# Conditioning products moved from TensorE to multiply-adds on VectorE, and the second upward piece by token blocks

## Chip, cores and metric

One core of one Trainium2 chip. The time is that of the program on the device, in microseconds (us), the median of several runs.

## What is computed

Two networks, one behind the other, on 256 tokens of width 1024, in float32. The first has a recurrent layer (a gated linear recurrence), an MLP, a layer of sparse attention with a latent key (an index score picks 64 keys a query), and a second MLP. The second is a hybrid layer (neighbourhood attention with context keys, a short convolution, a conformer branch), whose input is shifted and scaled by a vector computed from a condition `c`, and whose output is gated by one:

```
def sq_relu_mlp(h, w_up, w_down):
    return jnp.square(jax.nn.relu(h @ w_up)) @ w_down        # 1024 -> 4096 -> 1024

def modulate(x, cond, norm_g, w_ada, b_ada):
    shift, scale, gate = jnp.split(jax.nn.silu(cond) @ w_ada + b_ada, 3, axis=-1)
    ...
    return rms_norm_2(x, norm_g) * (1 + scale) + shift, gate

x = x + mix                                                  # in each layer of the first network
x = x + sq_relu_mlp(rms_norm(x, norm_mlp_g[layer]), mlp_w_up[layer], mlp_w_down[layer])
```

The conditioning is `silu(cond) @ w_ada`, a row vector of 1024 times a 1024 x 3072 matrix. It is needed for two conditions (tokens and context) for shift and scale, and for one (tokens) for the gate. It depends on nothing but the inputs, and its result is first used in the second MLP, where the context is normalised.

## The kernel before

All weights come from HBM in pieces of 1 MB ([128, 2048] in float32), in one order written out by hand (`order()`). SP's queue loads them into a ring of three buffers (`RAW`). Each piece is split into a rounded part `WH` (ScalarE, `high`, L1104) and the remainder `WL` (VectorE, `low`, L1708), in a second ring of four. TensorE multiplies in three products (high by high, high by low, low by high), so that the result keeps float32 accuracy: `columns_matmul` (L294 to L296, weights stationary, 256 tokens moving), `tokens_matmul` (L325 to L327, a block `t` of 128 tokens stationary) and `columns_wide` (L312, L314).

An MLP has 16 upward pieces of 256 hidden columns and 16 downward pieces. In iteration j TensorE makes upward piece j and adds downward piece j - 2 to four PSUM banks (`t`, `n`: token block and half of the columns). ScalarE copies (L1254), VectorE adds, squares and makes the remainder (L1960, L1964, L1970).

Between stages the residual is added (`residual`, L1742), its squares summed on ScalarE (`norm_square`, L1111), the mean square made on VectorE (`variance`, L1718) and raised to -0.5 on GpSimd (`power`, L2520), the block scaled (`norm_scaled`, L1727), transposed on TensorE (`norm_transposes`, L364, the *turning* of a token block) and split again (`norm_high` L1140 on ScalarE, `norm_low` L1736 on VectorE). `residual_norm` and `norm_stage` hold VectorE's and ScalarE's order of this.

The conditioning matrix is taken in twelve pieces of 1 MB, four before each of three stages: the first MLP, attention and the second MLP. TensorE multiplies them in plain float32 (`ada_matmul`, L392): the condition's 128 values, padded to 32 columns, are the stationary operand, and a piece's 2048 columns move in four products of 512 to four groups of 32 output partitions. Ten of the pieces pass through the ring `RAW`, two are loaded ahead into `AD`. A copy to `AR` and small products with a selecting matrix (`ada_columns`, L405) turn the row to columns, and VectorE adds the bias (`ada_out`).

The first upward piece of an MLP is multiplied by token blocks (`up_by_tokens`), so that block 0 can start before block 1 is normalised; its hidden tile must then be transposed (`S.turn`, L546). The others are multiplied by `columns_matmul` (piece 1) and `columns_wide`. `rows_last_two` writes the last sum of a stage, block by block. In attention, `dots` (L661) makes the index scores, and `key_weights` (L675, copied at L1355) transposes the key weights between them.

Of the kernel before, what the change touches and what calls it, by code (L numbers as in the profile page):

```python
# [18 lines left out]
def order():  # L19
# [31 lines left out]
    return p  # L51

# [33 lines left out]

AHEAD = [("ada", 1, 0), ("ada", 1, 1)]


def chunks():  # L90
    out, i, m, at = {}, 0, 0, 0
    for key, piece in order():
        whole = key[0] in ("ada", "ri")
        apart = key[0] == "ri" or key in AHEAD
        out[key] = Chunk(None if apart else i, None if whole else m, piece[0], at)
        i += 0 if apart else 1
        m += 0 if whole else 1
        at += 128 * WIDTH[piece[0]]
    return out
# [38 lines left out]
class Memory:  # L138
# [3 lines left out]
    def __init__(self, nc, stack):  # L142
# [30 lines left out]
        self.TB = self.tile("TB", [128, 2, 512])  # L173
        self.AD = self.tile("AD", [128, 2, 2048])

# [47 lines left out]
        self.CM = self.tile("CM", [128, 8, 32])  # L223
# [117 lines left out]
def rows_last_two(T, M, S, stage, keys, x, ks, xready):  # L341
# [40 lines left out]
def ada_matmul(T, M, S, g, i, bank):  # L382
    c = M.CH["ada", g, i]
    if (g, i) in ((1, 0), (1, 1)):
        T.wait_ge(S.ahead[i], 16)
        weights = M.AD[:, i, :]
    else:
        T.wait_ge(S.raw[c.r], 16 * (c.i // NRAW + 1))
        weights = M.RAW[:, c.r, :]
    for q in range(4):  # L390
        k = 4 * g + i if g < 2 else 2 * i + q // 2
        made = T.e.matmul(M.PS[bank][32 * q:32 * q + 32, :], M.CM[:, k, :], weights[:, q * 512:(q + 1) * 512],  # L392
                          start=i == 0, stop=i == 3)
    made.then_inc(*S.ada.tick(g, i))


def ada_columns(T, M, S, g, bank):
    T.wait_ge(*S.arow.at(0))
    T.wait_ge(*S.arow.at(g))
    T.wait_ge(S.rest, 16)  # L400
    sel, n = (("sel", 8), ("selg", 4), ("selg", 4))[g - 1] if g == 1 else ("selg", 4)
    which = (0, 1) if g == 1 else (0,)
    for m in range(4):
        for a in which:
# [110 lines left out]
def tensor_mlp(T, M, S, l):  # L515
# [33 lines left out]
    if l:  # L549
        T.wait_ge(*S.xl.at(k, 1, 0))  # L550
        ada_columns(T, M, S, 2, 6)
# [2525 lines left out]
```

## Time and profile before

| | |
|---|---|
| median of 3 runs | 880.0 us (879.88 to 880.57) |
| the profiled execution | 879.89 us, its span 878.1 us |
| TensorE busy | 872.1 us of the span |
| VectorE, ScalarE, GpSimd busy | 588.9, 467.0, 65.0 us |
| read from HBM | 162.92 MB, 187 GB/s over the span |
| conditioning products on TensorE (L392) | 96 records, between 94.3 and 394 us |

The span runs from the first to the last instruction; the execution's own time has 1.8 us around it. Busy times are those of engines that work side by side, so they do not add up. Matmuls of TensorE overlap in the records; the distance of their starts is what one costs in a full row.

### The profile page before, as it was taken

The numbers are of one execution on the slowest core, as the hardware profiler recorded it, in microseconds if no ns is written. First come the engines' busy times: TensorE is split into PE (matmuls) and PEld (weight loads), VectorE is DVE, ScalarE is ACT, GpSimd is POOL, SyncE is SP. The second block draws the span as 40 slices with busy tenths as digits, with TensorE's granted clock in tenths as the row PEclk, the third lists the DMA queues.
The fourth block names the chain that finished last, engine by engine and source line by source line (L and its number), as shares of the span: only waits on it lengthen the run. The fifth ranks groups of instructions, "written<-read, shape, count | busy, mean of one in ns | idle before, by whom it ended". The sixth has DMA issues, their size and how long they took to land.

```text
span 878.1 us, 13080 instructions
## 1 busy us (share of the span) xinstructions
PE 872.1 (99%) x5128; PEld 742.8 (85%) x5128; DVE 588.9 (67%) x981; ACT 467.0 (53%) x749; POOL 65.0 (7%) x71
## 2 busy tenths in 40 slices
PE   9999999999999999999999999999999999999998
PEld 7998788888887887679888888888898888878887
DVE  5969775555554495567648576564477898896874
ACT  6796554444433477646546544454467674444540
POOL 3010000000000045300000000031100000000000
PEclk9999999999999999999999999999999999999999
DMA  8635886665542644478537455520435355545431
GB/s 326 241 124 208 304 293 242 243 237 195 192 144 97 228 171 166 137 267 328 188 116 278 185 192 192 192 108 8 188 110 182 126 196 189 189 150 200 171 155 48
DMA packets 30447, 164.81 MB, mean 188 GB/s; under 512 B 3377, under 2 KB 9777, under 8 KB 12082
## 3 DMA queue, kind: packets, MB, share of 16 engines
q1 hardware_dynamic: 30384, 163.97, 51.2%
q8 instruction: 41, 0.67, 0.3%
q14 instruction: 20, 0.16, 0.1%
q10 hardware_dynamic: 2, 0.00, 0.0%
HBM read 162.92 MB, written 1.05 MB: 187 GB/s over the span
## 4 chain that ended last, share of the span: by engine, by line
PE 97%; ACT 1%; DMA 1%; DVE 0%; issue 0%; SPq 0%; DVEq 0%; ACTq 0%
PE ps L325 16%; PE ps L327 16%; PE ps L326 16%; PE ps L312 12%; PE ps L294 7%; PE ps L295 7%; PE ps L296 7%; PE ps L314 6%; PE ps L466 2%; PE ps L392 1%; PE ps L887 1%; PE ps L912 1%; PE ps L896 1%; DMA BI<-in_dbias_dram 1%; PE ps L364 1%; ACT LG L1372 1%
## 5 line engine op out<-in xcount | busy, mean ns | idle before, releaser
L1708 DVE TENSOR_TENSOR WL<-RAW,WH 128x1024 fp32r<-128x1024 f32 x258 | 304.2, 1217 | 86.1 <-ACT WH L1104 85.7
L1104 ACT CAST WH<-RAW 128x1024 fp32r<-128x1024 f32 (+1 forms) x264 | 262.6, 1044 | 77.0 <-PE ps L327 66.7
L294 PE MATMUL ps<-XA,WH 128*128 128x256 f32 x496 | 143.3, 289 | 0.1
L312 PE MATMUL ps<-XA,WH 128*128 128x512 f32 x448 | 140.6, 395 | 0.0
L296 PE MATMUL ps<-XA,WL 128*128 128x256 f32 x496 | 140.3, 283 | 0.0
L295 PE MATMUL ps<-XA,WH 128*128 128x256 f32 x496 | 140.3, 283 | 0.0
L294 PEld LDWEIGHTS ps<-XA,WH 128*128 128x128 f32 x496 | 95.0, 192 | 7.4 <-issue 6.5
L314 PEld LDWEIGHTS ps<-XA,WL 128*128 128x128 f32 x448 | 84.2, 188 | 19.6
L325 PE MATMUL ps<-WH,HTh 128*128 128x512 f32 x256 | 100.0, 390 | 0.0
L326 PE MATMUL ps<-WL,HTh 128*128 128x512 f32 x256 | 99.7, 389 | 0.0
L327 PE MATMUL ps<-WH,HTl 128*128 128x512 f32 x256 | 99.6, 389 | 0.0
L295 PEld LDWEIGHTS ps<-XA,WH 128*128 128x128 f32 x496 | 95.1, 192 | 0.4 <-issue 0.2
L296 PEld LDWEIGHTS ps<-XA,WL 128*128 128x128 f32 x496 | 95.0, 192 | 0.0
L314 PE MATMUL ps<-XA,WL 128*128 128x256 f32 x448 | 88.0, 278 | 0.0
L312 PEld LDWEIGHTS ps<-XA,WH 128*128 128x128 f32 x448 | 70.2, 189 | 2.0
L325 PE MATMUL ps<-WH,XA 128*128 128x512 f32 (+2 forms) x192 | 71.2, 371 | 0.2
L327 PE MATMUL ps<-WH,XA 128*128 128x512 f32 (+2 forms) x192 | 69.7, 363 | 0.0
L326 PE MATMUL ps<-WL,XA 128*128 128x512 f32 (+2 forms) x192 | 69.7, 363 | 0.0
L1254 ACT COPY RL<-ps 128x512 f32<-128x512 f32 x28 | 16.4, 587 | 89.9 <-PE ps L314 89.8
L1960 DVE TENSOR_TENSOR RL<-ps,RL 128x512 f32<-128x512 f32 x28 | 19.4, 692 | 65.6 <-ACT RL L1254 65.6
L327 PEld LDWEIGHTS ps<-WH,HTl 128*128 128x128 f32 x256 | 48.1, 188 | 10.2
L325 PEld LDWEIGHTS ps<-WH,HTh 128*128 128x128 f32 x256 | 48.0, 188 | 9.0
(272 smaller groups left out, 1293.2 us busy)
## 6 DMA issues: line engine op xcount, KB each, us to landing
RAW<-in_w_dram SPq DMA_DIRECT2D x139, 1024.0 KB, 4.8
RI<-in_w_dram SPq DMA_DIRECT2D x2, 1024.0 KB, 11.3
GB<-in_gb_dram SPq DMA_DIRECT2D x4, 512.0 KB, 5.7
AD<-in_w_dram SPq DMA_DIRECT2D x2, 1024.0 KB, 6.8
BI<-in_dbias_dram SPq DMA_DIRECT2D x16, 128.0 KB, 4.6
NB<-in_nbias_dram SPq DMA_DIRECT2D x16, 128.0 KB, 2.1
RAW<-in_w_dram SPq DMA_DIRECT2D x2, 528.0 KB, 4.2
X<-in_x_dram SPq DMA_DIRECT2D x2, 512.0 KB, 4.0
```

The costliest lines, as they stand in the source:

```text
L294: T.e.matmul(dst, h, xh[:, k, :], start=k == 0, stop=False)
L295: T.e.matmul(dst, h, xl[:, k, :], start=False, stop=False)
L296: last = T.e.matmul(dst, l, xh[:, k, :], start=False, stop=k == 7)
L312: T.e.matmul(M.PS[bank + m][:, :], parts[i][0], M.X2[:, k + i, :], start=k + i == 0, stop=False)
L314: last = T.e.matmul(M.PS[bank + m][:, 0:256], parts[i][1], M.XA[0][:, k + i, :], start=False, stop=k + i == 7)
L325: T.e.matmul(dst, a, h, start=first and j == 0, stop=False)
L326: T.e.matmul(dst, a, l, start=False, stop=False)
L327: made = T.e.matmul(dst, b, h, start=False, stop=last and j == len(pairs) - 1)
L466: made = T.e.matmul(M.PS[b][:, m * 256:(m + 1) * 256], M.RI[:, blk // 2, col:col + 128], M.XC[:, 2 * blk + kk, :], start=kk == 0, stop=kk ...
L1104: A.e.copy(M.WH[:, c.s, sl], M.RAW[:, c.r, sl]).then_inc(*S.hi.tick(key, a))
L1708: D.e.tensor_tensor(M.WL[:, c.s, sl], M.RAW[:, c.r, sl], M.WH[:, c.s, sl].bitcast(F32), ALU.subtract).then_inc(*S.lo.tick(key, a))
L1960: D.e.tensor_tensor(r, M.banks[:, b:b + 2, 0:256], r, ALU.add).then_inc(*S.up.tick(l, j))
```

## The change

The conditioning products are taken off TensorE. VectorE multiplies each half piece ([128, 1024]) by the condition's column, one scalar for each partition, and adds it to an accumulator `AD` (`ada_sums`): for the first MLP 8 pieces, two conditions, 32 operations in iterations 1 to 13; for the second MLP 4 pieces, one condition, 8 operations in iterations 3 to 10. What is left for TensorE is one sum over the 128 partitions (`ada_rows`, a column of ones as the stationary operand): eight products of 512 columns at the entry of attention, four of 256 at the entry of the last stage. The loads have three buffers of their own, outside the ring, and stand in SP's queue ahead of the upward pieces that `ADA_LOADS` names.

Both of the first two upward pieces go by token blocks, with two hidden tiles to turn. The first token block is turned ahead of the very last group of the last sum (`between`, `turned`). The order of the splits and norms on VectorE and ScalarE changes with it. The key weights are transposed at the entry of attention.

```
-        p += up[:2] + [(("ada", 2 * layer, k), ("D" if layer else "A", "w_ada_2", 0, k)) for k in range(4)]
+        p += [(("ada", layer, k), ("D" if layer else "A", "w_ada_2", 0, k)) for k in range(4 if layer else 8)]
+        p += up[:2]
...
-            p += [(("ada", 1, k), ("A", "w_ada_2", 0, 4 + k)) for k in range(4)]
...
+ADA_STEPS = [{j: (1, 2 - j % 2) for j in range(1, 14)}, {j: (0, 1) for j in range(3, 11)}]
+ADA_LOADS = [{2: (0, 1, 2), 5: (3,), 6: (4,), 7: (5,), 8: (6, 7), 9: (8,), 10: (9,), 11: (10,), 12: (11, 12), 13: (13,), 14: (14,), 15: (15,)},
+             {3: (0, 1, 2), 7: (3,), 8: (4,), 9: (5,), 10: (6,), 11: (7,)}]
...
 rows_last_two(T, M, S, stage, keys, x, ks, xready, between):
                 xready(q)
+                if (t, n, q) == (1, 1, 1):
+                    between()
                 made = rows_group(T, M, S, key, x, ks[q], t, n, False, q == 1)
...
+def ada_rows(T, M, S, l, bank):
+    n = 256 if l else 512
+    T.wait_ge(*S.zeros.at("on"))
+    T.wait_ge(*S.adacc.at(l, *ada_order(l)[-1]))
+    for which in range(1 if l else 2):
+        for q in range(4):
+            made = T.e.matmul(M.PS[bank][32 * q:32 * q + 32, 0:n], M.EO[:, which, :], M.AD[:, which, q * n:(q + 1) * n],
+                              start=which == 0, stop=l == 1 or which == 1)
+    made.then_inc(*S.ada.tick("rows", l))
...
 def tensor_mlp(T, M, S, l):
-    ada_matmul(T, M, S, g, 0, 5)
-    norm_transposes(T, M, S, k, 0)
-    ada_matmul(T, M, S, g, 1, 5)
-    up_by_tokens(T, M, S, l, 0)
+    up_by_tokens(T, M, S, l, 0, 0)
+    up_by_tokens(T, M, S, l, 1, 0, halves=(0,))
     norm_transposes(T, M, S, k, 1)
-    ada_matmul(T, M, S, g, 2, 5)
-    ada_matmul(T, M, S, g, 3, 5)
-    up_by_tokens(T, M, S, l, 1).then_inc(*S.freed.tick("up", l, 0))
-    T.wait_ge(*S.arow.at(g))
-    columns_matmul(T, M, S, ("up", l, 1), M.XA, 5, xready).then_inc(*S.freed.tick("up", l, 1))
+    up_by_tokens(T, M, S, l, 1, 0, halves=(1,))
+    up_by_tokens(T, M, S, l, 0, 1).then_inc(*S.freed.tick("up", l, 0))
+    up_by_tokens(T, M, S, l, 1, 1).then_inc(*S.freed.tick("up", l, 1))
+    turn(0)
...
+        if j == 2:
+            turn(1)
...
+                if l == 0 and (t, n, j) == (1, 1, 15):
+                    T.wait_ge(*S.up.at(0, 15))
+                    norm_transposes(T, M, S, 2, 0)
...
 def tensor_dsa(T, M, S):
-    ada_matmul(T, M, S, 1, 0, 5)
-    norm_transposes(T, M, S, k, 0)
-    ada_matmul(T, M, S, 1, 1, 5)
+    ada_rows(T, M, S, 0, 5)
...
-    ada_matmul(T, M, S, 1, 2, 5)
-    ada_matmul(T, M, S, 1, 3, 5)
+    key_weights(0)
+    key_weights(1)
...
 def tensor_second(T, M, S):
+    take(6)
+    ada_rows(T, M, S, 1, 6)
     tokens("nk", M.XB, 2, 0, 0, cready)
+    ada_columns(T, M, S, 1, 6)
...
 def norm_stage(A, M, S, k, stage, second, third):
     norm_square(A, M, S, k, 0, 1, stage)
     high(A, M, S, *second, halves=(1,))
+    norm_high(A, M, S, k, 0)
     norm_square(A, M, S, k, 1, 0, stage)
-    norm_high(A, M, S, k, 0)
     norm_square(A, M, S, k, 1, 1, stage)
+    high(A, M, S, *third)
     norm_high(A, M, S, k, 1)
...
 def residual_norm(D, M, S, stage, last, k, first, second, third):
     residual(D, M, S, stage, last, 0, 0)
-    low(D, M, S, *first)
+    low(D, M, S, *first, halves=(0,))
     residual(D, M, S, stage, last, 0, 1)
-    low(D, M, S, *second)
     variance(D, M, S, k, 0)
+    low(D, M, S, *first, halves=(1,))
+    norm_scaled(D, M, S, k, 0)
     residual(D, M, S, stage, last, 1, 0)
-    norm_scaled(D, M, S, k, 0)
+    norm_low(D, M, S, k, 0)
     residual(D, M, S, stage, last, 1, 1)
-    norm_low(D, M, S, k, 0)
+    low(D, M, S, *second, halves=(0,))
     variance(D, M, S, k, 1)
+    low(D, M, S, *second, halves=(1,))
     norm_scaled(D, M, S, k, 1)
+    low(D, M, S, *third, halves=(0,))
     norm_low(D, M, S, k, 1)
+    low(D, M, S, *third, halves=(1,))
...
+def ada_sums(D, M, S, l, left, n):
+    for key in left[:n]:
+        i, half, which = key
+        at = 2 * i + half
+        D.wait_ge(S.aw[at % 3], 16 * (at // 3 + 1 + (len(range(at % 3, 16, 3)) if l else 0)))
+        src = M.AWS[l][at % 3]
+        k = 2 * i + half if l else i
+        col = 0 if l else half * 1024
+        dst = M.AD[:, which, col:col + 1024]
+        scalar = M.CM[:, k, which:which + 1]
+        if k == 0:
...
+            made = D.e.tensor_scalar(dst, src, scalar, None, ALU.mult)
+        else:
+            D.wait_ge(*S.adacc.at(l, *ada_prior(l, *key)))
+            made = D.e.scalar_tensor_tensor(out=dst, in0=src, scalar=scalar, in1=dst, op0=ALU.mult, op1=ALU.add)
+        made.then_inc(*S.adacc.tick(l, *key))
+    del left[:n]
...
+    def conditioning(l, at):
+        i, half = at // 2, at % 2
+        if at >= 3:
+            before = (l, (at - 3) // 2, (at - 3) % 2)
+            Y.wait_ge(*S.adacc.at(*before, 0 if l else 1))
+        c = M.CH["ada", l, i]
+        src = D["w"][c.at:c.at + 128 * 2048].rearrange("(p n) -> p n", p=128)
+        Y.e.dma_start(M.AWS[l][at % 3], src[:, half * 1024:(half + 1) * 1024]).then_inc(S.aw[at % 3], 16)
```

In an iteration j of an MLP, VectorE calls `ada_sums` twice: behind the square of tile j (the first number of `ADA_STEPS`), and behind the remainder of tile j, ahead of that of downward piece j (the second). In the last stage ScalarE copies the gate's row sums (`AR`) behind the squares of the first block.

## Rows read from the trace of the kernel before

**Rows 1.** The page, busy time of each engine.
```profile
PE 872.1 (99%) x5128; PEld 742.8 (85%) x5128; DVE 588.9 (67%) x981; ACT 467.0 (53%) x749; POOL 65.0 (7%) x71
```
**Rows 2.** The chain that ended last, in order of time: start, length in us.
```profile
94.13 0.23 PE ps L327
```
**Rows 3.** Waits of TensorE: total us, times, longest.
```profile
PE ps L726 <- ACT PT L1379: 0.6, 1, 0.6
```
**Rows 4.** Timeline of TensorE, entry of the first MLP: start, length in us.
```profile
94.29 1.06 PE L392 MATMUL ps<-RAW,CM 128*32 128x512 f32 x8
95.28 1.09 PE L364 MATMUL ps<-CP,XN 128*128 128x128 f32 x8
96.31 1.06 PE L392 MATMUL ps<-RAW,CM 128*32 128x512 f32 x8
97.43 0.36 PE L325 MATMUL ps<-WH,XA 128*128 128x256 f32 x1
...
100.38 1.04 PE L364 MATMUL ps<-CP,XN 128*128 128x128 f32 x8
101.35 1.92 PE L392 MATMUL ps<-RAW,CM 128*32 128x512 f32 x16
103.20 0.39 PE L325 MATMUL ps<-WH,XA 128*128 128x256 f32 x1
```
**Rows 5.** Timeline of TensorE, attention's entry.
```profile
295.26 1.85 PE L405 MATMUL ps<-CP,AR 128*128 128x8 f32 x16
296.96 0.31 PE L645 MATMUL ps<-CP,KC 128*128 128x128 f32 x1
```
**Rows 6.** Timeline of all engines, index dots in attention.
```profile
303.28 0.93 PE L661 MATMUL ps<-KI,QI 64*128 64x128 f32 x8
304.13 0.66 PE L675 MATMUL ps<-CP,UK 128*128 128x128 f32 x4
...
305.01 0.59 ACT L1355 COPY UKT<-ps 128x512 f32<-128x512 f32 x1
...
305.48 0.62 ACT L1344 COPY QI<-ps 128x512 f32<-128x512 f32 x1
...
306.17 0.93 PE L661 MATMUL ps<-KI,QI 64*128 64x128 f32 x8
```
**Rows 7.** Timeline of ScalarE, residual's second half squared, first MLP's entry.
```profile
90.37 0.19 ACT L1111 ACTIVATION_READ_ACCUMULATOR J<-X 128x1 f32 x1
```
**Rows 8.** Timeline of GpSimd and VectorE, norms at 275 and 573 us.
```profile
275.14 0.55 POOL L2520 TENSOR_TENSOR ST<-ST,NH 128x1 f32<-128x1 f32 x1 [176.50 <-DVE ST L1718]
...
573.40 0.21 DVE L1718 TENSOR_SCALAR ST<-ST 128x1 f32<-128x1 f32 x1 [0.34 <-ACT J L1111]
...
573.53 1.21 DVE L1708 TENSOR_TENSOR WL<-RAW,WH 128x1024 fp32r<-128x1024 f32 x1
573.69 1.46 POOL L2520 TENSOR_TENSOR ST<-ST,NH 128x1 f32<-128x1 f32 x1 [5.57 <-DVE ST L1718]
...
575.18 0.75 DVE L2123 SCALAR_TENSOR_TENSOR X<-X,ST,GB 128x512 f32<-128x512 f32 x1 [0.44 <-POOL ST L2520]
```
**Rows 9.** Timeline of VectorE, one iteration of the first MLP; one of thirteen.
```profile
151.82 0.69 DVE L1960 TENSOR_TENSOR RL<-ps,RL 128x512 f32<-128x512 f32 x1 [2.69 <-ACT RL L1254]
...
157.78 2.36 DVE L1708 TENSOR_TENSOR WL<-RAW,WH 128x1024 fp32r<-128x1024 f32 x2 [1.68 <-ACT WH L1104]
162.83 0.69 DVE L1960 TENSOR_TENSOR RL<-ps,RL 128x512 f32<-128x512 f32 x1 [2.69 <-ACT RL L1254]
```
**Rows 10.** Windows: busy us by engine, clock, DMA share, GB/s, same iteration.
```profile
149.00:160.00 11.00, 11.00 (x58) 9.35 (x57) 6.60 (x8) 5.00 (x6) 0.00 (x0) 1.00 0.74 279
```
**Rows 11.** Instructions of lines L1727 and L1708: min/median/max ns.
```profile
L1727 DVE SCALAR_TENSOR_TENSOR XN<-X,ST,GB x12: 743/749/753, 93.6 to 390.2; 128x512 f32<-128x512 f32 x12
...
L1708 DVE TENSOR_TENSOR WL<-RAW,WH x258: 700/1219/2145, 16.8 to 860.1; 128x1024 fp32r<-128x1024 f32 x127, 128x528 fp32r<-128x528 f32 x2
```
**Rows 12.** DMA issues by line: KB each, median us to landing.
```profile
AD<-in_w_dram SPq DMA_DIRECT2D x2, 1024.0 KB, 6.8
```

More of the change, by code:

```diff
@@ L93, in chunks @@
         whole = key[0] in ("ada", "ri")
-        apart = key[0] == "ri" or key in AHEAD
-        out[key] = Chunk(None if apart else i, None if whole else m, piece[0], at)
-        i += 0 if apart else 1
+        out[key] = Chunk(None if whole else i, None if whole else m, piece[0], at)
+        i += 0 if whole else 1
         m += 0 if whole else 1
@@ L379, in first_transposes, with ada_columns @@
         made.then_inc(*S.tr.tick(0, t, n))
[L382 to L398, printed above, removed]
-    T.wait_ge(*S.arow.at(g))
-    T.wait_ge(S.rest, 16)
[L401 to L404, printed above, removed]
-            made = T.e.matmul(M.PS[bank][:, n * m:n * m + n], M.AR[:, a, m * 128:(m + 1) * 128], M.cc(sel, 0, n),
-                              start=a == 0, stop=a == which[-1])
-    made.then_inc(*S.adacols.tick(g))
+def ada_rows(T, M, S, l, bank):
[7 more added lines that the diff above has]
+    made.then_inc(*S.ada.tick("rows", l))
+def ada_columns(T, M, S, l, bank):
+    T.wait_ge(*S.arow.at(l))
+    T.wait_ge(S.rest, 16)
+    for m in range(2 if l else 4):
+        made = T.e.matmul(M.PS[bank][:, 8 * m:8 * m + 8], M.AR[:, l, m * 128:(m + 1) * 128], M.cc("sel", 0, 8), start=True, stop=True)
+    made.then_inc(*S.ada.tick("columns", l))
 def tensor_rec(T, M, S):
@@ L1119, in norm_square, with norm_stage @@
     square_sum(A, M, S, M.X[:, t, n * 512:(n + 1) * 512], 1.0 / 32, k, t, n)
-def norm_stage(A, M, S, k, stage, second):
+def norm_stage(A, M, S, k, stage, second, third):
     norm_square(A, M, S, k, 0, 0, stage)
@@ L1486, in scalar_second @@
     squares(0)
+    A.wait_ge(*S.ada.at("rows", 1))
+    A.e.copy(M.AR[:, 1, 0:256], M.PS[6][:, 0:256]).then_inc(*S.arow.tick(1))
     high(A, M, S, "nv", 0)
@@ L2587, in chunk @@
         prior = M.ORDER[c.i - NRAW] if c.i >= NRAW else None
[L2588 to L2592 removed]
+        if prior is not None:
             Y.wait_ge(*S.hi.at(prior, 1))
@@ L2676, in sync_program @@
             bias(h)
-    for key in M.ORDER[M.ORDER.index(("ada", 2, 0)):M.ORDER.index(("nk", 0))]:
-        if key == ("ada", 2, 1):
+    for key in M.ORDER[M.ORDER.index(("up", 1, 2)):M.ORDER.index(("nk", 0))]:
+        if key == ("up", 1, 3):
             gain(4)
+        for at in ADA_LOADS[1].get(key[2], ()) if key[:2] == ("up", 1) else ():
+            if at == 0:
+                Y.wait_ge(*S.pv.at(7))
+            conditioning(1, at)
         if key == ("up", 1, 4):
@@ L2739, in signals @@
     S.g, S.bi = [landed(f"g{i}") for i in range(2)], [landed(f"bi{i}") for i in range(4)]
-    S.ahead = [landed(f"ahead{i}") for i in range(2)]
+    S.aw = [landed(f"aw{i}") for i in range(3)]
     S.cx, S.nb = [landed(f"cx{t}") for t in range(2)], [landed(f"nb{i}") for i in range(2)]
@@ L2757, in signals @@
     S.ri = count("ri", [(blk, which) for blk in blocks for which in range(2)])
-    S.ada = count("ada", [(g, i) for g in range(3) for i in range(4)])
-    S.adacols, S.turn = count("adacols", [1, 2]), count("turn", layers)
+    S.ada = count("ada", [(what, l) for l in layers for what in ("rows", "columns")])
+    S.turn = count("turn", [(l, j) for l in layers for j in range(2)])
     S.ctr, S.ftr = count("ctr", TN), count("ftr", TN)
```

216 lines of the change are left out of this document (107 added, 109 removed).

## The prediction

> **What bounds the kernel now.** I read the page first: busy shares, then the chain that ended last. TensorE is busy for 99% of the span [rows 1] and nearly all of the chain is its own, product behind product at 0.23 us for 512 columns [rows 2], at a granted clock of full speed (2.4 GHz, the upper of its two levels). In the list of waits its longest for another engine, after the first microseconds, is the 0.6 of [rows 3]. So this kernel is a row of TensorE instructions without holes. A gain is TensorE time taken out, less the holes that open where that work had stood. VectorE, at 67%, has room, if not at each moment.
>
> Then the timeline where the conditioning runs, at the entry of the first MLP [rows 4]. The reader should look at the starts, since matmuls overlap and their lengths say less. Four conditioning pieces of four products (eight records each) go 8 records in 0.99 us (94.29 to 95.28) and 16 in 1.85 (101.35 to 103.20). Between them stand the two turnings (eight transposes each, 1.03 us) of the normalised blocks. The pieces do work and also fill time in which VectorE and ScalarE prepare the next block. The two other places, at attention's entry and the second MLP's, repeat this to 0.1 us.
>
> **What is removed from TensorE.** From the first piece to the token products 3.14 us pass (94.29 to 97.43), from the second turning on 2.82 (100.38 to 103.20): 5.96 in all, 2.06 of it the two turnings, which stay. So 3.90 us of pieces go at each of three places, 11.7 in all. The small products that turn rows to columns halve: sixteen records took 1.70 us [rows 5], so eight take 0.85; the gate's eight, 0.85 by the same row, leave the second MLP, and four, 0.4, stand in the last stage.
>
> **What is added to TensorE.** (1) The sums over partitions of the first 2048 columns: eight products of 512 columns, sixteen records, as 101.35 to 103.20: 1.85, and 0.15, an estimate, for the changes between plain and rounded operands on both sides (in the chain the pieces start 0.1 us later than a further product of the sum would). (2) Those of the gate: four products of 256 columns. Not in the trace. Half of eight records of 512 columns is 0.5; if the columns did not matter it is 0.93. I take 0.6, nearer to the half, since the price of the wide ones is the same in blocks of four. (3) A second turning of a hidden tile in each MLP: four transposes, half of the 1.03 of eight [rows 4], 0.54 with the changes, twice. (4) The second upward piece by token blocks: 48 products of 256 columns either way, 24 of which took 2.95 (97.43 to 100.38); nothing. (5) The key weights' eight transposes move from between the dots to the attention entry, at 0.6 for four (0.66 long in [rows 6], less the overlap): 1.18 there. They had covered a wait: the third dots need the second index queries, which ScalarE copies behind two ReLUs. In [rows 6] the copy starts at 305.48, behind one key-weight copy that goes; from 305.01 it would end at 305.6, so the third dots start at about 305.7, 2.42 after the first in place of 2.89 (303.28 to 306.17). That saves 0.47 for 1.18 spent: a net loss of 0.71, of which 0.7 is a hole. If the copy's wait were not there the saving would be 1.2; if ScalarE is a further 0.6 late, nothing.
>
> **The turnings.** The first one now stands ahead of the very last group of the last sum, so its inputs are due one group (six products, 1.36 us) earlier. At the first MLP the last sum ends at 94.2 to 94.3 [rows 2, 4], its last block (twelve products) begins at 91.5, and the turning is wanted at 92.9. The chain: the square of the residual's second half ends at 90.56 [rows 7], the mean square starts at 90.7. GpSimd then raises it to a power. VectorE now runs half a weight remainder in that interval. The trace has both cases: with the addition out of PSUM behind the mean square (the order now) GpSimd took 0.55; beside a weight remainder, which reads two tiles of SBUF, it took 1.46 and held the normalisation to 1.78 us after the mean square (573.40 to 575.18) [rows 8]. So the normalisation starts at 92.5 and its halves of 0.75 [rows 11] end at 93.2 and 93.9; with 0.1 to be seen, TensorE starts the second four transposes at 94.0 in place of 93.45: a hole of 0.55. The bounds are nothing, with GpSimd at 0.55 (halves done by 93.4), and 1.5 us, if the remainder and GpSimd go one after the other twice. The attention layer's exit has the same distances. Between MLP and attention the remainder is of 528 columns instead of 1024, half as long, and the hole closes.
> The Trainium skill (GPSIMD Engine Reference, Specifications) says that GpSimd shares its SBUF interfaces with VectorE and contends with instructions of two SBUF inputs. The 1.46 against 0.55 agrees, and this rule speaks against the new order of VectorE's queue; were there no such contention, the two holes of 0.55 would be nothing and the sum 8.1 us in place of 7.0.
> The second turning comes 4.4 us after the last sum (24 products, then 12). The addition starts 0.2 behind that sum, with 0.6 for itself, then a half remainder, 1.14 start to start (two in 2.36, one in 1.22 [rows 9, 11]), the mean square at 1.94, the normalisation at 3.7, its halves done at 4.5 and 5.1, where TensorE asks at 4.5 and 5.0: a hole of 0.15, between nothing and 0.6. At the attention entry the 1.86 of the sums stands ahead, so no hole. Behind a turned half come a copy on ScalarE and a remainder on VectorE, of 512 columns, 0.6 to 0.7 each as those of [rows 6, 9]; the products that read them stand a group of 1.36 or more behind, though a half remainder of the third piece is queued ahead of the second. Behind ScalarE's wait for the first turning now stand the squares of the second block, which are due only after.
>
> **What moves to VectorE and to the queues.** One iteration of the MLP's loop takes 11.01 us of TensorE (151.82 to 162.83) and VectorE is busy for 6.60 of it, with holes of 2.69 and 1.68 [rows 9, 10]. The first MLP gets 32 multiply-adds of 1024 columns, two or three an iteration. One of 512 columns with two tiles and a column operand took 0.75 and a remainder of 1024 goes at 1.14 start to start, 1.22 in all [rows 11], so I take 1.2: three are 3.6 and make 10.2, below 11.01; two make 9.0. Even the start, where the second hidden tile waits for the new turning and VectorE falls some 4 us behind, is made good in three iterations. From the end of upward piece j to the products that read its tile and weights pass one and a half iterations, 16.5 us; VectorE has them ready within 10, so a lag of 4 costs nothing. The point at which it costs is a mean multiply-add of 1.8 us ((11.01 - 6.5) / 2.5). The second MLP gets eight, one an iteration. The loads (16 halves of 0.5 MB, then 8) stand in SP's queue ahead of upward pieces. Each waits for the sum that frees its buffer, made in the iteration before the wait on the ring that follows it anyway; a piece of twice that size landed in 6.8 us [rows 12] and each is first used an iteration later. An iteration's 2 MB of weights (190 GB/s) become 2.7 in the mean (250) and 3 at most (285), what [rows 10] already moves at a share of 0.74. The ring no longer carries conditioning, so the loads around the entries are earlier. In the last stage ScalarE waits for the gate's sums ahead of a weight piece and the second block's squares, some 3 us later than now (an estimate: sums, copy, and the weight piece behind instead of ahead); the transposes that these feed stand behind three groups of 24 products, 5.4 us each.
>
> **The sum.** First MLP: 3.90 - 0.54 - 0.55 - 0.15 = 2.66. Attention: 3.90 - 2.00 + 0.85 - 0.71 = 2.04. Second MLP: 3.90 - 0.54 - 0.70 + 0.85 = 3.51. Last stage: -0.6 - 0.4 - 0.2 = -1.2. Together 7.0 us less. The profiled execution took 879.89 (span 878.1), so 872.9; the median of the runs is 880.0, 0.1 above it: 873.0.
>
> **The rivals.** (A) The turnings find their inputs in time and the dots don't wait: 1.4 of holes and 0.7 less: 871. For it: the holes are tenths, built from chains of ten steps. Chance 0.14. (B) The norm chain is what the pieces had covered. All six turnings wait 1 us, 6.0 in place of 1.4: 877.6. If each entry loses as much as was taken out, 880. For it: without the pieces nothing else fills. Against: the token products of a whole second piece now do, and the first turning is covered by the last group. Chances 0.10 and 0.05. (C) The gain before attention's softmax is given back there, where ScalarE holds TensorE once already (0.6 [rows 3]): the 2.0 of that entry is lost: 875. Against: VectorE's scores start 0.5 to 0.7 earlier too, since two copies leave ScalarE's queue. Chance 0.05. (D) The other side: VectorE sets the pace of the first MLP. If a multiply-add takes 2.15, as the longest weight remainder did [rows 11], 2.5 of them add 5.4 to 6.5: 11.9 an iteration, 0.9 more than TensorE needs, thirteen times 11.7: 884. It decides from 1.8 us on. Against: the 2.15 is one of 258, and GpSimd is idle in this stage (0.00 in [rows 10]). Chance 0.05. The forecast keeps 0.61.
>
> **How the numbers follow.** The likeliest is 873.0, its own range 871.5 to 874.5. To leave out 2 in 10 the range takes in most of A (down to 870.6) and C (up to 876.0). Some 0.2%, 1.8 us, is what a measurement of this kernel can tell from no change. Forecast, A, C and most of B lie below 878.2: faster 0.90. The rest of B: within 0.05. D: slower 0.05.
>
> **What would show it.** TensorE records down by the 96 of the pieces, plus 24 of the new sums; the starts at each entry with last group, eight transposes, last group, then token products without a stretch of conditioning; holes of 0.5 ahead of the first turning's second half in the MLPs, GpSimd's power at 1.4 there; loop iterations still 11.01 with VectorE at 9 to 10.2 busy; third dots 2.4 behind the first. Wrong is the forecast if iterations in the first MLP exceed 11.01, if TensorE waits for a weight remainder or a conditioning sum, or if a turning waits over 1 us.

## The result and the profile after

The changed kernel takes 871.14 us (median of four runs, 870.80 to 871.34), the one before 879.94 beside it: a ratio of 0.9899 (95% interval 0.9882 to 0.9916), 8.8 us less. Forecast were 873.0, with a range of 870.6 to 876.0. The profiled execution took 871.34 (span 869.5); the span before was 878.1, so 8.6 is to be found in the traces.

The page, busy time (after), to be held against [rows 1]:
```profile
PE 862.9 (99%) x5052; PEld 741.3 (85%) x5052; DVE 634.3 (73%) x1023; ACT 466.4 (54%) x748; POOL 73.8 (8%) x71
```
TensorE is still the bound, with 9.2 us less of work and 76 records fewer: 96 of the pieces out, 24 of the sums in, 12 of the small products out, 8 of the second turnings in. VectorE has 45 us more and nobody waits for it in the loops.

TensorE's waits (after): total, times, longest.
```profile
PE ps L427 <- DVE AR L1824: 1.5, 1, 1.5
PE ps L676 <- ACT QI L1357: 0.8, 1, 0.8
PE ps L386 <- DVE XN L1736: 0.4, 2, 0.2
PE ps L400 <- DVE XN L1839: 0.3, 1, 0.3
PE ps L345 <- DVE XA L1745: 0.2, 1, 0.2
PE ps L731 <- POOL LG L2601: 0.2, 1, 0.2
```
L386 are the turnings of the norms: the holes forecast are there, and small. L676 are the third dots. The wait of [rows 3] is gone, which was not forecast.

TensorE's timeline (after), entry of the first MLP, answering to [rows 4]:
```profile
93.78 1.23 PE L386 MATMUL ps<-CP,XN 128*128 128x128 f32 x8 [0.19 <-DVE XN L1736]
94.76 0.47 PE L345 MATMUL ps<-WH,XBh 128*128 128x512 f32 x1
...
96.23 0.28 PE L345 MATMUL ps<-WH,XA 128*128 128x256 f32 x1
...
109.12 0.60 PE L544 MATMUL ps<-CP,SQ 128*128 128x128 f32 x4
109.47 0.71 PE L332 MATMUL ps<-XA,WH 128*128 128x512 f32 x2
```
The turning stands ahead of the last group (94.76), and token products follow it at once. A hidden tile's turning takes 0.35 (109.12 to 109.47).

VectorE and GpSimd there, around the first normalisation (after):
```profile
91.03 0.21 DVE L1727 TENSOR_SCALAR ST<-ST 128x1 f32<-128x1 f32 x1 [0.79 <-ACT J L1125]
91.16 1.21 DVE L1717 TENSOR_TENSOR WL<-RAW,WH 128x1024 fp32r<-128x1024 f32 x1
92.89 1.41 DVE L1736 SCALAR_TENSOR_TENSOR XN<-X,ST,GB 128x512 f32<-128x512 f32 x2 [0.51 <-issue]
```
```profile
91.33 1.46 POOL L2567 TENSOR_TENSOR ST<-ST,NH 128x1 f32<-128x1 f32 x1 [31.47 <-DVE ST L1727]
```
GpSimd's power takes the 1.46 of [rows 8], and the normalisation starts 1.86 after the mean square (forecast 1.8).

Windows over two neighbouring iterations of the first MLP (after), as [rows 10]:
```profile
150.90:161.91 11.01, 11.01 (x57) 9.37 (x56) 8.92 (x10) 5.01 (x7) 0.00 (x0) 1.00 0.93 319
161.91:172.92 11.01, 11.01 (x57) 9.37 (x56) 10.11 (x11) 5.00 (x7) 0.00 (x0) 1.00 0.70 246
```
TensorE has no hole in 11.01; VectorE is busy for 8.92 with two sums and 10.11 with three, so a sum costs 1.19 (forecast 1.2, 9.0 and 10.2).

**Where the 8.6 us are.** Stretches between equal points of the two timelines, in us:

| stretch | before | after | saved | forecast |
|---|---|---|---|---|
| start to the first column product | 18.13 | 18.74 | -0.6 | 0 |
| to the first downward product, first MLP | 99.83 | 96.75 | 3.1 | 2.66 |
| to attention's first queries | 196.70 | 194.31 | 2.4 | 2.04 |
| to the first downward product, second MLP | 95.04 | 89.90 | 5.1 | 3.51 |
| to the end of its last sum | 161.33 | 161.44 | -0.1 | 0 |
| last stage, to the first head's turning | 16.33 | 17.58 | -1.25 | -1.2 |
| to the end | 290.74 | 290.78 | 0 | 0 |

Of the 5.1, 1.15 lie in the softmax, where two waits of TensorE are gone, and 4.0 at the MLP's entry. The prediction has no term for two of these, the -0.6 and the 1.15.

### The profile page after: what moved, and what is told of

Same layout as the page of the kernel before. It is cut to its first block, busy times and chain, and to the rows that moved or that the text cites. A ratio compares the mean times of both kernels' runs of the same rounds, so it can differ in the third digit from the quotient of the medians.

```text
span 869.5 us, 13006 instructions
## 1 busy us (share of the span) xinstructions
PE 862.9 (99%) x5052; PEld 741.3 (85%) x5052; DVE 634.3 (73%) x1023; ACT 466.4 (54%) x748; POOL 73.8 (8%) x71
## 3 DMA queue, kind: packets, MB, share of 16 engines
HBM read 162.92 MB, written 1.05 MB: 189 GB/s over the span
## 4 chain that ended last, share of the span: by engine, by line
PE 96%; DVE 2%; POOL 1%; ACT 1%; issue 0%; DVEq 0%
PE ps L345 16%; PE ps L347 16%; PE ps L346 16%; PE ps L332 12%; PE ps L314 7%; PE ps L316 6%; PE ps L315 6%; PE ps L334 6%; PE ps L480 2%; PE ps L901 1%; PE ps L926 1%; PE ps L910 1%; PE ps L386 1%; PE ps L746 1%; PE ps L723 1%; POOL ST L2567 1%
## 5 line engine op out<-in xcount | busy, mean ns | idle before, releaser
L314 PE MATMUL ps<-XA,WH 128*128 128x256 f32 x464 | 134.2, 289 | 0.1
L316 PE MATMUL ps<-XA,WL 128*128 128x256 f32 x464 | 131.3, 283 | 0.0
L315 PE MATMUL ps<-XA,WH 128*128 128x256 f32 x464 | 131.2, 283 | 0.0
L334 PEld LDWEIGHTS ps<-XA,WL 128*128 128x128 f32 x448 | 84.1, 188 | 19.6
L314 PEld LDWEIGHTS ps<-XA,WH 128*128 128x128 f32 x464 | 88.9, 192 | 7.4 <-issue 6.5
L315 PEld LDWEIGHTS ps<-XA,WH 128*128 128x128 f32 x464 | 88.9, 192 | 0.4 <-issue 0.2
L316 PEld LDWEIGHTS ps<-XA,WL 128*128 128x128 f32 x464 | 88.9, 192 | 0.0
L334 PE MATMUL ps<-XA,WL 128*128 128x256 f32 x448 | 88.0, 278 | 0.0
L345 PE MATMUL ps<-WH,XA 128*128 128x512 f32 (+2 forms) x224 | 80.1, 357 | 0.2 <-DVE XA L1745 0.2
L347 PE MATMUL ps<-WH,XA 128*128 128x512 f32 (+2 forms) x224 | 78.7, 351 | 0.0
L346 PE MATMUL ps<-WL,XA 128*128 128x512 f32 (+2 forms) x224 | 78.7, 351 | 0.0
L332 PEld LDWEIGHTS ps<-XA,WH 128*128 128x128 f32 x448 | 70.2, 189 | 2.0
L347 PEld LDWEIGHTS ps<-WH,HTl 128*128 128x128 f32 x256 | 48.1, 188 | 10.2
L346 PEld LDWEIGHTS ps<-WL,HTh 128*128 128x128 f32 x256 | 48.1, 188 | 8.9
```

The costliest lines, as they stand in the source:

```text
L314: T.e.matmul(dst, h, xh[:, k, :], start=k == 0, stop=False)
L315: T.e.matmul(dst, h, xl[:, k, :], start=False, stop=False)
L316: last = T.e.matmul(dst, l, xh[:, k, :], start=False, stop=k == 7)
L332: T.e.matmul(M.PS[bank + m][:, :], parts[i][0], M.X2[:, k + i, :], start=k + i == 0, stop=False)
L334: last = T.e.matmul(M.PS[bank + m][:, 0:256], parts[i][1], M.XA[0][:, k + i, :], start=False, stop=k + i == 7)
L345: T.e.matmul(dst, a, h, start=first and j == 0, stop=False)
```

## The experiments

Twelve runs follow, two of them of unchanged kernels, with the kernel before measured beside each (medians 880.38 to 880.47). The changed kernel itself, run again, took 871.41; "slower" and "faster" below are against it. Edits are made to the changed kernel; times are medians, ratios are to the kernel before.

**1 and 2. The two kernels once more (after_again, before_again).**

> The changed kernel once more, unchanged, beside the three below on one chip, since they differ from it by tenths: 871.1 to 871.3. In its trace the first product of the first layer may start anywhere from 18.1 to 20.5, if that is chance; VectorE's wait for the second heads' biases is again near 2 (3 in both traces of the kernel before).

> The kernel before once more, unchanged, for a second trace. Two differences between the traces lie outside what the prediction forecast. (1) VectorE's wait for the biases of the second heads, 3.06 before and 1.8 to 2.0 after, with 1.16 of TensorE's waits behind it: if it belongs to the change (loads in another order), this trace shows about 3 again; if it is chance of a transfer, it may show 2. (2) The first product of the first layer at 18.13 before and 18.74 to 20.5 in traces with the change: if it is chance, this trace may show any value between; if it belongs to the change, 18.1 again.

after_again: 871.41 (871.33 to 871.49), ratio 0.9900 (0.9885 to 0.9915), first column product at 18.73. before_again: one run of 879.73, first product at 18.09. VectorE in the softmax, in the second trace of before:
```profile
348.31 0.29 DVE L2085 CUSTOM_DVE_ANT_0 LG<-ps,BI 128x128 f32<-128x128 f32 x1 [2.98 <-DMA BI<-in_dbias_dram]
```
and in the changed kernel's first:
```profile
342.33 0.29 DVE L2131 CUSTOM_DVE_ANT_0 LG<-ps,BI 128x128 f32<-128x128 f32 x1 [1.77 <-DMA BI<-in_dbias_dram]
```
The reader should look at the brackets. This is head 8 (of heads 0 to 15), the first of the third four, and its wait for the biases is 3.06 and 2.98 in the two traces of before, 1.76 to 2.00 in all twelve that have the change. Behind the long one TensorE falls back by 0.4 and 0.75 at two softmax products (by the starts of the same products in the two timelines), and the wait of [rows 3] is the larger of the two. So the 1.15 belongs to the change. Why is open. SP issues these loads at the same distance from TensorE's work in both kernels (4.86 apart, as everything there). A head's biases come in two transfers, and VectorE waits for both. The first of head 8 lands 4.57 and 4.67 after its issue in before and 4.41 to 4.73 with the change; the second 5.80 and 5.73 in before, and 4.51 to 4.75 in all twelve. So it is the second alone that comes 1.0 to 1.3 earlier, and no run here takes the reason apart.

**3. The first turning behind the last sum (turn_behind).**
```diff
-                if (t, n, q) == (1, 1, 1):
-                    between()
...
     rows_last_two(T, M, S, "rec", ..., turned)
+    turned()
```
Likewise for the second MLP; in attention it stands ahead of the sums over partitions.

> The first turning of each norm goes back behind the last group of the last sum, everything else is as in the changed kernel (871.1). My theory: in the MLPs the turning then finds its inputs (the hole of 0.25 ahead of it goes), but behind it nothing covers the copy and the remainder: the first four transposes 0.54, the copy 0.6, the remainder 0.65, 0.1 to be seen make 1.9 us from its start, and its eight transposes last 1.03, so a hole of 0.85 at each MLP; 0.4 to 0.6 net each, since the second turning then comes later and its hole of 0.22 goes as well. At attention the sums over partitions (1.86) stand behind the turning and cover it: nothing. Together 0.8 to 1.2 slower than the changed kernel: 872.1. Rival B of the prediction (the pieces had covered the norm chain and nothing else does): 1 us at each of six turnings, 875 or more.

873.64 (873.20 to 874.95), ratio 0.9924 (0.9910 to 0.9937): 2.2 slower, twice what I expected. TensorE's waits in it:
```profile
PE ps L345 <- DVE XA L1744: 2.3, 3, 1.1
...
PE ps L345 <- ACT WH L1117: 0.6, 1, 0.6
```
The token products wait 1.06 for the copy and remainder in the first MLP and 1.05 in the second, where 0.85 was expected, and the stretches there are 0.8 and 0.9 longer, where 0.4 to 0.6 was. The rest of the miss is attention, 0.8 where I had expected nothing: ScalarE's copies of the first turned block stand in its queue ahead of the squares of the second and of the next weight pieces, so a late turning makes a weight piece late as well (0.58, `ACT WH`). The early turning saves more than its own chain.

**4. The second turning one half piece earlier (turn_early).**
```diff
     up_by_tokens(T, M, S, l, 0, 0)
-    up_by_tokens(T, M, S, l, 1, 0, halves=(0,))
     norm_transposes(T, M, S, k, 1)
-    up_by_tokens(T, M, S, l, 1, 0, halves=(1,))
+    up_by_tokens(T, M, S, l, 1, 0)
```

> In the changed kernel the second turning of each MLP stands behind 36 token products of the first two upward pieces (24 of the first, 12 of the second) and waits 0.22 for its input; here it stands behind 24, and the 12 follow it. If those 12 products are what gave the norm chain its time, the turning is asked for 1.45 earlier while its input comes at the same moment: the hole grows from 0.22 to 1.67 at each MLP, nothing is gained behind it, 2.9 slower than the changed kernel: 874.1. Rival: part of the chain moves with TensorE (the last sum frees the residual's blocks at the same time, so it should not), less than 1 slower. Rival B of the prediction (even now the chain is what TensorE waits for, so moving the work behind the turning only trades places): same time.

874.04 (873.91 to 874.32), ratio 0.9929 (0.9914 to 0.9943). TensorE's timeline, first MLP:
```profile
100.78 1.32 PE L386 MATMUL ps<-CP,XN 128*128 128x128 f32 x8 [1.51 <-DVE XN L1735]
```
The turning starts at the same 100.78 as in the changed kernel (100.77): its input does not move, and the twelve products that had filled the time until then come behind. The two stretches are 1.46 and 1.53 longer. This is the cleanest test of rival B: the norm chain needs cover, and what covers it now are the token products of the second piece by blocks, worth about 1.5 at each MLP by the traces and 1.3 by the medians. That the pieces had covered it before is read from VectorE's timeline of the kernel before, where the block is normalised:
```profile
98.68 1.41 DVE L1727 SCALAR_TENSOR_TENSOR XN<-X,ST,GB 128x512 f32<-128x512 f32 x2 [0.67 <-POOL ST L2520]
```
Its halves end at 99.4 and 100.1, and the turning starts at 100.38 [rows 4]: without the two pieces ahead of it, 0.99 each, it would have been asked for at 98.4, before either was ready (an estimate from these rows).

**5. Seven of the eight sums over partitions left out (rows_out).** In `ada_rows(0)` only one product is made; the conditioning is then not the reference's.

> At attention's entry seven of the eight products that sum the conditioning over partitions are left out (fourteen of sixteen records, 1.62 us); the output is not the reference's. Theory that these sums also cover the norm chain there, as the pieces had: the second turning is asked for 1.62 earlier (279.4 by the changed kernel's trace), while its normalised halves are ready at 279.7 and 280.4: its end comes only 0.8 to 0.9 earlier, the rest is given back as a hole: 0.8 faster than the changed kernel. Rival, that they only cost what they last: 1.6 faster.

871.01 (870.49 to 871.95), ratio 0.9899 (0.9882 to 0.9915): 0.4 faster by the medians, less than the spread of these runs, of 1.62 taken out; so the reading rests on the trace. TensorE's timeline:
```profile
273.35 1.06 PE L386 MATMUL ps<-CP,XN 128*128 128x128 f32 x8
275.73 1.04 PE L413 MATMUL ps<-AD,EO 128*32 128x512 f32 x2
280.03 1.04 PE L386 MATMUL ps<-CP,XN 128*128 128x128 f32 x8
```
From the first turning to the second pass 6.68, against 7.24 with all the sums: 0.56 less, and 1.06 given back, as the token products start only at 276.71 (some 0.7) and their second half at 278.51 (0.3). So two thirds of the sums' TensorE time at this place is cover, and a further cut there is worth a third of its length.

**6 and 7. A weight remainder behind the normalisation (lows_behind, lows_first).**
```diff
-    low(D, M, S, *first, halves=(1,))
     norm_scaled(D, M, S, k, 0)
+    low(D, M, S, *first, halves=(1,))
```
lows_behind does the same for the second block, at all three entries; lows_first only this, and only in the MLPs.

> At the three places the second half of a weight remainder is moved behind the normalisation of the block, so that VectorE does nothing while GpSimd takes the power. Theory that GpSimd contends with VectorE's two-operand reads: GpSimd's power takes 0.55 instead of 1.46, the normalisation starts 0.95 after the mean square instead of 1.86, and the four holes of 0.22 to 0.25 ahead of the turnings in the MLPs go: 0.9 faster than the changed kernel, 870.2. Rival that the power is slow for another reason and VectorE's own occupation is not the limit: it still takes 1.46 and the time is the same, 871.1. Second rival, the weight half is now late for the products that read it: a wait of 0.1 to 0.5 at each place takes the gain back, 871.1 to 871.6.

> As lows_behind, but only where it paid in that trace: the second half of the first weight remainder behind the first block's normalisation, in the two MLPs only. There the first turning starts without a hole, 0.3 earlier at each (93.44 for 93.78), and the products behind it kept the gain (95.88 for 96.23). Theory: 0.3 twice, less up to 0.2 twice at the second turning, whose input then is what is awaited: 0.2 to 0.6 faster than the changed kernel, at the edge of what can be measured. Rival: the second turning's input does not move, so all of it is given back there: same time.

lows_behind: 872.89 (872.33 to 874.87), ratio 0.9916 (0.9903 to 0.9930), 1.5 slower. Its GpSimd and VectorE in the first MLP, to be held against the rows of after above:
```profile
91.33 0.55 POOL L2567 TENSOR_TENSOR ST<-ST,NH 128x1 f32<-128x1 f32 x1 [31.47 <-DVE ST L1727]
```
```profile
91.98 1.42 DVE L1736 SCALAR_TENSOR_TENSOR XN<-X,ST,GB 128x512 f32<-128x512 f32 x2 [0.73 <-POOL ST L2567]
93.31 1.22 DVE L1717 TENSOR_TENSOR WL<-RAW,WH 128x1024 fp32r<-128x1024 f32 x1
```
The mechanism is shown: the power starts at the same 91.33 and takes 0.55 instead of 1.46, the normalisation starts 0.91 earlier, and the turning at 93.44 for 93.78. The Trainium skill (SBUF — State Buffer, Who interferes with whom) says that a VectorE instruction with two SBUF inputs contends with a GpSimd instruction that reads SBUF, and that the ports they share are an exclusive lock. The trace agrees with the lock too: in the changed kernel the remainder ends at 92.37 and the power 0.42 later, nearly the whole of its 0.55. But the gain was given back. In the MLPs TensorE waits 0.26 and 0.25 for the weight remainder that was put behind at the second block, and both stretches are as long as in the changed kernel. Its wait in attention:
```profile
280.95 0.36 PE L345 MATMUL ps<-WH,XA 128*128 128x264 f32 x1 [1.29 <-DVE WL L1717]
```
There the remainder that I put behind is needed first. lows_first, without that place: 870.60 (870.35 to 870.99), ratio 0.9891 (0.9876 to 0.9906), 0.8 faster by the medians; its trace accounts for 0.36 (0.2 at the first MLP's entry, 0.16 at the second's), and the rest is an earlier first product (18.17 for 18.73), see 9. So only the 0.36 can be put down to the edit. The second turnings still wait 0.15 for their input, as their power still runs beside a remainder.

**8. ScalarE's copy ahead of its ReLUs (copy_ahead).**
```diff
+    evict(S.qiev, M.QI, 1, 2, "qi", 1)
     rlh(0)
     rlh(1)
-    evict(S.qiev, M.QI, 1, 2, "qi", 1)
```

> ScalarE's copy of the second index queries stands ahead of its first ReLU instead of behind the second. In the changed kernel the third dots wait 0.8 for it, and ScalarE idles for 6 us before the first ReLU. If that queue order is the cause of the hole, the third dots start 1.6 behind the first (2.37 now) and the keys and values behind them move up: 0.8 faster, 870.3. Rival: the fourth dots need the second ReLU, which then ends later in relation to them, and the wait moves there: 0.0 to 0.4 faster. Second rival: the 0.8 is given back at the softmax, where VectorE's scores and masks are what is late: same as the changed kernel.

870.38 (869.80 to 872.01), ratio 0.9887 (0.9874 to 0.9901). TensorE from the first dots to the keys, first in the changed kernel:
```profile
298.93 1.58 PE L676 MATMUL ps<-KI,QI 64*128 64x128 f32 x16
301.30 0.93 PE L676 MATMUL ps<-KI,QI 64*128 64x128 f32 x8 [0.80 <-ACT QI L1357]
302.16 1.13 PE L691 MATMUL ps<-CT,UKT 128*128 128x256 f32 x4
```
then with the copy ahead:
```profile
300.60 2.24 PE L676 MATMUL ps<-KI,QI 64*128 64x128 f32 x24
302.76 1.13 PE L691 MATMUL ps<-CT,UKT 128*128 128x256 f32 x4
```
3.23 become 2.16: 1.07 gained, and the medians show 1.0. The runs spread more than the changed kernel's: the profiled one took 872.01, with its first column product at 20.47 in place of 18.73, which is another matter (see 9). The hole was ScalarE's queue order: it had idled for 6 us ahead of the first ReLU, and the copy's input was there when the first dots began.

**9. GpSimd's first remainder behind VectorE's scaling (start_apart).**
```diff
     power(0, 1)
+    P.wait_ge(*S.xn.at(0, 1, 1))
     low_by_pool("xr", 0)
```

> In the changed kernel's trace TensorE is 0.6 later than in the kernel before at the first product of the first layer (18.74 against 18.13): VectorE's two scalings of the second block took 2.98 together instead of 0.88, while GpSimd ran its weight remainder from 9.04 on (10.07 before). Here GpSimd's remainder waits until the scaling is done. Theory that the two contend: the scaling takes 0.88 again, the remainder starts near 9.75, and the first product is back at 18.1: 0.6 faster, 870.5. Rival, that the 0.6 is chance of one execution (the weights landed a microsecond earlier in it): the time of the runs does not change, 871.1. Second rival: GpSimd's remainder is then what TensorE waits for: same or slower.

871.34 (871.31 to 871.39), ratio 0.9895 (0.9882 to 0.9909): the same time, so the two contend as the theory says, but that is not what the 0.6 comes from. VectorE in the changed kernel and in this one:
```profile
8.83 2.98 DVE L1839 TENSOR_SCALAR XN<-X,ST 128x512 f32<-128x512 f32 x2 [0.68 <-POOL ST L2567]
```
```profile
8.83 0.88 DVE L1839 TENSOR_SCALAR XN<-X,ST 128x512 f32<-128x512 f32 x2 [0.68 <-POOL ST L2567]
```
The collision is real, and gone, yet the first column product is at 18.74 again; after_again, where it did not happen either, has 18.73. TensorE's sixteen turnings there took 3.62 (TensorE's timeline of this kernel) against 2.60 in before:
```profile
8.83 3.62 PE L400 MATMUL ps<-CP,XN 128*128 128x128 f32 x16
```
The transposes come at 0.21 each for a while and then at 0.11, and the moment of the change differs between executions. It is the moment at which the clock record of each trace begins, with a granted clock of 1.00 (the upper level, 2.4 GHz): 10.23 and 10.13 in before, 10.13 to 16.25 with the change, 13.12 here. No row says what was granted ahead of it (a window there reads 1.00 only because no record says otherwise), so that it was the lower level is read from the pace alone: in sums_double below, where the record has the lower level for a stretch, products take about twice as long as well. The first column product follows that moment. It comes at 18.1 to 18.2 where the record begins at 10.1 to 10.3 (five traces, both of before among them), at 18.32 for 10.61, at 18.73 or 18.74 for 11.5 to 13.1 (six traces, the changed kernel's first among them), and at 19.93 and 20.47 for 15.0 and 16.25. The collision needs first weights that land early, at 7.36 to 8.07 in the five traces that have it, at 8.27 or later in those without it and without this edit. In three of the five GpSimd started between the two scalings (9.04 to 9.22), and the first product came at 18.17, 18.32 and 18.74, no later than without; in the other two it started ahead of both (8.76), and these are the two late starts. Whether it was the collision that put the clock's rise off there is open.

The two traces of before are of its faster executions (879.73 and 879.89): its runs go from 879.46 to 880.66, and one took 881.92. So the -0.6 of the table is most likely chance of an execution and no cost of the change.

**10 and 11. More VectorE work per sum (sums_half_more, sums_double).**
```diff
+            if l == 0:
+                D.wait_ge(*S.adx.made_so_far())
+                D.e.scalar_tensor_tensor(out=M.XN[:, 0, 0:w], in0=src[:, 0:w], scalar=scalar, in1=dst[:, 0:w],
+                                         op0=ALU.mult, op1=ALU.add).then_inc(*S.adx.tick(*key))
+                D.wait_ge(*S.adx.at(*key))
             made = D.e.scalar_tensor_tensor(out=dst, in0=src, scalar=scalar, in1=dst, op0=ALU.mult, op1=ALU.add)
```
w is 512 in the one and 1024 in the other. The tile `XN` is not in use there. 28 of the 32 sums have such a second operation (the first four only multiply, and have none), not the 31 that I expected. The two waits around it are for VectorE's own last one; with them it takes 0.78 start to start in the one and 1.31 in the other.

> Each of the first MLP's multiply-adds gets a second one of 512 columns beside it that writes to an unused tile: 1.19 + 0.75 = 1.94 us of VectorE for each. VectorE without sums is busy for 6.6 of an iteration's 11.01, and two or three sums fall into one: 10.5 in some and 12.4 in the others. By the prediction's threshold (a mean sum of 1.8) this is just over: the mean iteration would be 6.6 + 2.46 x 1.94 = 11.4, 0.4 over TensorE's, thirteen times 5 slower if the lag is not absorbed; with the slack of some 6 us that tiles and weights have, 0 to 2 slower than the changed kernel, 871 to 873. Rival: VectorE has hidden room (waits in it can be filled), same time. Rival: its queue order, not its sum, decides, and TensorE waits in each iteration of three: 1.4 x 7 = 10 slower.

> Each of the first MLP's multiply-adds is done twice (the second writes to an unused tile), 2.4 us of VectorE each. 31 of them add 31 x 1.2 = 37 us. By the prediction's rule the iterations become 6.6 + 2.46 x 2.4 = 12.5 in the mean in place of 11.01: 13 x 1.5 = 19.5, less a slack of some 6: 13 to 20 slower than the changed kernel, 884 to 891. Rival, that the sums are hidden whatever they take: same time. Rival, that contention with the loads from memory sets in as well: more than 25 slower.

sums_half_more: 871.18 (870.76 to 873.00), ratio 0.9900 (0.9885 to 0.9914), no change. Windows of eleven us in its first MLP:
```profile
129.00:140.00 11.00, 11.00 (x57) 9.35 (x56) 10.89 (x13) 5.12 (x6) 0.00 (x0) 1.00 0.78 282
162.00:173.00 11.00, 11.00 (x58) 9.36 (x57) 10.86 (x13) 5.12 (x6) 0.00 (x0) 1.00 0.71 266
```
VectorE hardly rests (10.89 of 11.00) and falls behind in each iteration: measured from the first column product, its last sum starts 8.0 later than in the changed kernel. TensorE feels nothing. sums_double: 884.54 (884.46 to 884.67), ratio 1.0047 (1.0030 to 1.0064), slower than the kernel before. Its windows:
```profile
162.00:173.00 11.00, 11.00 (x58) 9.35 (x57) 10.89 (x11) 5.00 (x6) 0.00 (x0) 1.00 0.69 242
195.00:206.00 11.00, 9.32 (x49) 7.79 (x47) 10.89 (x11) 4.25 (x5) 0.00 (x0) 1.00 0.58 222
228.00:239.00 11.00, 8.27 (x32) 6.63 (x32) 10.89 (x11) 4.63 (x6) 0.00 (x0) 0.84 0.46 168
```
For a good six iterations the lag grows unseen, then TensorE waits, seven times, 9.8 in all and up to 2.7 at once, for weight remainders and the last time for ScalarE's rounding of a hidden tile. Behind the second wait of 2.7, which ends at 232.58, the granted clock is at its lower level (1.2 GHz) from 233.41 to 236.82, which makes the 0.84 of the last window; products of 512 columns come at 0.43 there in place of 0.23, eight of them, so 1.6 is the clock's. How much lag is free can be read from the two timelines: when TensorE first waits (0.16 at 193.03), VectorE's remainders and sums start 12.5 later than in the changed kernel, and at the last sum they are 22.9 behind it, TensorE itself 9.1. So 12 to 14 lie ready ahead of TensorE, twice the 6 that I expected. Rival D's mechanism exists, but its threshold was set too low: at 1.97 us a sum (1.19 and 0.78) the lag of 8.0 still cost nothing. The sum itself measured 1.19.

**12. Edits of 6, 8 and 9 together (three_edits).**

> copy_ahead, lows_first and start_apart together. If they add: 0.8 for the dots, 0.2 to 0.6 for the turnings, and none of the starts in which VectorE's scaling runs beside GpSimd (1 us in some executions): 1.0 to 1.4 faster than the changed kernel, 869.9, and a smaller spread of the runs. Rival: only the dots count, 870.4.

869.73 (869.34 to 869.91), ratio 0.9880 (0.9865 to 0.9895): 1.7 faster than the changed kernel on the same chip, whose runs (871.33 to 871.49) do not overlap these. By its trace 1.07 are the dots and 0.36 the turnings, the rest a first product at 18.16. Its first weights landed at 7.82, earlier than in the changed kernel's first trace (7.89), where GpSimd collided with the scaling; here it waited, and the scaling took 0.88. It is the fastest version found.

## Why the prediction was right, point by point

**The bound.** TensorE's row of instructions, less what opens as holes: right. What VectorE took over (45 us of it) cost TensorE nothing, and experiments 10 and 11 show how far off the edge was: at 1.97 a sum nothing changes, at 2.5 it costs 13.1. The prediction had put the edge at 1.8 a sum, and 1.97 is still free.

**The pieces, 3.90 a place.** Right. At the first MLP 3.90 less one tile's turning (0.35), a hole of 0.34 and one of 0.22 make 3.0, and 3.1 were saved. No run takes the pieces off TensorE and leaves the rest as it was; their worth is read from the stretches.

**Additions.** The sums took 1.86 (276.12 to 277.98), without the 0.15 for changes of operand; the gate's 0.57 (561.23 to 561.80; forecast 0.6), the small products 0.81 and 0.36 (0.85, 0.4), the key weights 1.22 (1.18), a wait of 0.18 behind them included. A hidden tile's turning was over-sized, 0.35 for 0.54: the changes of operand that I added do not show. That is 0.19 of each MLP's surplus of 0.4 to 0.5; the smaller holes give 0.14.

**The turnings.** The mechanism was right to the tenth (power 1.46, normalisation 1.86 after the mean square) and experiments 6 and 7 show that GpSimd beside the remainder is its cause. The hole was mis-sized: 0.34 (93.78 against 93.44 without the contention), not 0.55, since the mean square came 0.3 earlier in relation to the last sum than I had placed it. The second turning's was 0.22, not 0.15. Rival B fell for the reason given against it: experiments 3, 4 and 5 show that the chain did need cover, and has it.

**The dots.** Third dots 2.37 behind the first, forecast 2.42; up to the keys 3.23 for 3.74 before, so 0.51 saved for 1.22 spent, forecast 0.47 and 1.18. Right, and avoidable: with the copy ahead it would have been 1.58 for 1.22.

**The last stage.** 1.25 lost, forecast 1.2, and ScalarE's later chain hidden as said.

**What was missed.** I took the softmax as unchanged and looked there only for a loss (rival C). It gave 1.15, by a load that lands earlier, for a reason that stays open. With 0.3 to 0.5 more at each of the three entries that makes 2.4 more than forecast; the late start of the profiled execution takes 0.6 of it and the stretches at the end 0.15. The median lies 1.9 under the forecast. The terms at the entries were right in kind and near in size, while the 1.15 and the start have no term in the sum and partly cancel, so the final number owes something to chance. It is rival A's, but not by A's way: the holes and the wait of the dots were all there.

## What to carry to other kernels

When work is taken out of a bounding engine, ask at each place what chain ran under it, and put other work there: here twelve products moved ahead of one turning are worth 1.3 to 1.5 us, and a third of what is cut from a stretch that is cover comes through. Look at the queue of each helper for an instruction whose input has long been ready and that stands behind one that waits: one line moved on ScalarE gave 1.07 us. Move a contended VectorE instruction only where its result is not wanted next: the same edit kept 0.2 in one place and, by one wait of 1.3, lost 1.5 in another.

## What the runs showed of the hardware

- GpSimd's power of one column took 0.55 alone, 0.94 beside a VectorE remainder of 528 columns and 1.46 beside one of 1024: it ends 0.4 after the remainder, and is not slowed by a fixed share.
- It is held by a whole row of such VectorE instructions, not by one. Later in the changed kernel a power of the same form (0.55 in the kernel before) stands beside a sum of the conditioning and two remainders without a gap between them, and ends 0.41 after the last of the three:
```profile
472.77 3.79 POOL L2567 TENSOR_TENSOR ST<-ST,NH 128x1 f32<-128x1 f32 x1 [44.11 <-DVE ST L1727]
```
```profile
472.61 1.27 DVE L1976 SCALAR_TENSOR_TENSOR AD<-AD,CM 128x1024 f32<-128x1024 f32 x1
473.81 2.35 DVE L1717 TENSOR_TENSOR WL<-RAW,WH 128x1024 fp32r<-128x1024 f32 x2
```
  Nothing waits for this power at once, so it costs no time here; at an entry it would.
- The other way round, two VectorE scalings of 512 columns with one SBUF input took 2.96 to 3.02 beside a GpSimd remainder, 0.88 alone: they wait for the GpSimd instruction (9.04 to 11.53 in the changed kernel's trace, they end at 11.81).
- At the start of the program TensorE's transposes come at 0.21 each and then at 0.11. The change is where the trace's record of the granted clock begins, at 1.00, between 10.1 and 16.3 in fourteen traces; ahead of it TensorE had worked from 1.45 on, with no pause over 0.8. The first column product follows, from 18.1 to 20.5.
- After a wait of 2.7 in a row of products (sums_double) the granted clock fell to its lower level 0.8 after the products had gone on, for 3.4, and products of 512 columns took 0.43 in place of 0.23; after an equal wait 25.5 earlier it did not fall.
